# A kernel of three attention layers: normalising the outputs instead of the probabilities, with the inverse sums returned from DRAM

## The reference, cut to what matters

```
s = q @ k.T * scale                       # layer 1: masked, and one sink logit appended
p = softmax(s)                            # over the keys (and the sink)
o = p @ v
y = (o * silu(g)) @ w_o
```

## Time and profile before

| | |
|---|---|
| median of 3 runs | 1159.05 us (1158.66 to 1159.08) |
| profiled execution | 1159.5 us, its span 1157.7 us |
| TensorE busy | 1099.8 us (95%) |
| VectorE busy | 734.3 us (63%) |
| ScalarE busy | 649.0 us (56%) |
| GpSimd busy | 419.3 us (36%) |

### The profile page before, as it was taken

The page is one execution under the profiler, slowest core; times in us unless marked ns, Lnnn a source line. Parts: engine busy times, 40 slices in busy tenths (PEclk is TensorE's granted clock), DMA queues, the critical chain, the costliest instruction groups (busy, mean ns, idle before and its releaser), DMA issues.

```text
span 1157.7 us, 20235 instructions
## 1 busy us (share of the span) xinstructions
PE 1099.8 (95%) x7430; PEld 900.7 (78%) x7430; DVE 734.3 (63%) x1590; ACT 649.0 (56%) x1355; POOL 419.3 (36%) x513
## 2 busy tenths in 40 slices
PE   5999999999998899999899999999999999999996
PEld 2678778877885689877688887898878777888785
DVE  7575766676568625363787787745767775527745
ACT  5604555555556526643677777846567753457733
POOL 2633012212120334675400002416654326456781
PEclk9999999999999999999999999999999999999998
DMA  9741424322114521130201101053212403213112
GB/s 373 253 163 46 176 107 162 133 108 101 46 29 173 204 81 37 40 109 35 57 14 34 65 10 47 1 166 87 73 46 78 151 19 128 91 56 121 44 37 73
DMA packets 34253, 109.33 MB, mean 94 GB/s; under 512 B 4516, under 2 KB 7076, under 8 KB 33772
## 3 DMA queue, kind: packets, MB, share of 16 engines
q1 hardware_dynamic: 34156, 108.05, 27.7%
HBM read 101.39 MB, written 2.11 MB: 89 GB/s over the span
## 4 chain that ended last, share of the span: by engine, by line
PE 75%; DVE 12%; ACT 5%; issue 3%; POOL 2%; DMA 2%; SPq 1%; DVEq 0%; POOLq 0%; ACTq 0%
PE PS L677 31%; PE PS L660 15%; PE PS L794 8%; PE PS L782 7%; PE PS L983 6%; PE PS L1051 3%; DMA AF<-wstream 2%; PE PS L712 2%; DVE AD L2372 1%; ACT AF L1272 1%; DVE AF L2069 1%; POOL AR L2553 1%; DVE AR L2273 1%; PE PS L884 1%; PE PS L693 1%
## 5 line engine op out<-in xcount | busy, mean ns | idle before, releaser
L2553 POOL TENSOR_TENSOR AR<-AF,AR 128x256 fp32r<-128x256 f32 x396 | 304.5, 802 | 585.2 <-ACT AR L1152 585.2
L677 PE MATMUL PS<-AR 128*128 128x512 f32 (+1 forms) x2208 | 450.5, 360 | 4.7 <-POOL AR L2553 1.4
L677 PEld LDWEIGHTS PS<-AR 128*128 128x128 f32 x2208 | 364.0, 189 | 72.6 <-issue 10.5
L660 PE MATMUL PS<-AR 128*128 128x256 f32 (+4 forms) x1284 | 244.9, 327 | 6.7 <-ACT AF L1272 1.7
L660 PEld LDWEIGHTS PS<-AR 128*128 128x128 f32 (+1 forms) x1284 | 179.8, 190 | 41.7 <-issue 20.6
L1281 ACT ACTIVATE AF<-PS 128x512 f32<-128x512 f32 (+3 forms) x192 | 124.6, 649 | 100.0 <-PE PS L782 96.0
L1272 ACT ACTIVATE AF<-PS,AF 128x512 f32<-128x512 f32 (+3 forms) x192 | 140.8, 733 | 27.2 <-DVE AF L2349 18.3
L782 PE MATMUL PS<-AF 128*128 128x128 f32 x864 | 127.4, 274 | 8.4 <-DVE AF L1990 5.9
L782 PEld LDWEIGHTS PS<-AF 128*128 128x128 f32 x864 | 100.1, 140 | 32.9 <-issue 15.5
L1152 ACT ACTIVATE AR<-AF 128x1024 fp32r<-128x1024 f32 x99 | 103.3, 1052 | 35.3 <-PE PS L983 27.9
L794 PE MATMUL PS<-AF 128*64 128x128 f32 x1728 | 115.3, 278 | 3.4 <-DVE AF L1997 2.5
(11 more groups left out here) (216 smaller groups left out, 1147.2 us busy)
## 6 DMA issues: line engine op xcount, KB each, us to landing
AF<-wstream SPq DMA_DIRECT2D x171, 512.0 KB, 5.0
AF<-x_in SPq DMA_DIRECT2D x2, 1024.0 KB, 8.5
AD<-rows SPq DMA_DIRECT2D x4, 512.0 KB, 5.9
out<-AF SPq DMA_DIRECT2D x16, 128.0 KB, 1.9
AF<-AF SPq DMA_DIRECT2D x28, 64.0 KB, 2.0
AF<-rpb_band SPq DMA_DIRECT2D x8, 224.0 KB, 5.2
BIAS<-rpb_band SPq DMA_DIRECT2D x8, 224.0 KB, 4.7
AF<-ctx_in SPq DMA_DIRECT2D x1, 1024.0 KB, 5.5
```

Source lines behind the costliest of these rows:

```text
L660: mm = pe.matmul(out, stationary, moving, start=i == 0, stop=i == len(products) - 1)
L677: mm = pe.matmul(out[:, 0:t1 - t0], a, b, start=k == 0 and i == 0, stop=k == nk - 1 and i == 2)
L2553: ins = pool.tensor_tensor(w[:, 1, at:at + 256], raw(c)[:, at:at + 256], w[:, 0, at:at + 256].bitcast(F32), ALU.subtract)
```

## The change

In the first six pairs of layer 1 and the first seven of layer 2 (`N_LATE`) the probabilities are no longer normalised. TensorE turns the bare exponentials as soon as `exp_done` says that they are there. The sums of a pair are collected (`late_sums`): 2 x 6 columns in layer 1, 2 x 4 in layer 2. At the first step of the next pair VectorE adds the sinks' part and inverts them all (`invert_sums`). The outputs have the queries on the free axis, so the inverse sums, which are columns, must become rows: SyncE stores them to DRAM element by element (each column to 128 consecutive numbers), waits until they are there, and loads them back as rows spread over 64 partitions for each half of the pair (`spread_sums`). At the first step of the pair after that VectorE multiplies the gated output by those rows (`scale_output`); in layer 2 the one of pair 6 follows at the last step of pair 7. The high parts wait for `scaled`. In the other pairs nothing changes.

```diff
+N_LATE = {"A": 6, "B": 7, "C": 0}
...
+        SUMS_AT = {"A": LOC_[:, 5920:5992], "B": ROPE[:, 1, 0:48]}
+        SUMS_OF = {layer: [tiles(SUMS_AT[layer][:, 4 * n * i:], 2, 2, n) for i in range(3)] for layer, n in (("A", 6), ("B", 4))}
+        SUM_ROWS = {"A": R3[:, 3072:3840].bitcast(F32), "B": ROPE[:, 0, :]}
...
             def turn(n):
                 u = units[n]
-                pe.wait_ge(p_ready, n + 1)
+                if late(n):
+                    pe.wait_ge(exp_done, n + 1)
+                else:
+                    pe.wait_ge(p_ready, whole_at[n] + 1)
...
+                total, sunk = late_sums(n) if late(n) else (STAT[:, 2, i:i + 1], STAT[:, 3, i:i + 1])
...
-                               accum_out=STAT[:, 2, i:i + 1]).then_inc(exp_done, 1)
+                               accum_out=total).then_inc(exp_done, 1)
...
             def out_high_a(j):
                 act.wait_ge(o_read, 2 * j + 2)
+                if j < N_LATE["A"]:
+                    act.wait_ge(scaled, late_at("A", j) + 1)
...
             def out_high_b(j, part):
                 act.wait_ge(o_read, 16 + j + 1)
+                if j < N_LATE["B"]:
+                    act.wait_ge(scaled, late_at("B", j) + 1)
...
+            def invert_sums(layer, p):
+
+                dve.wait_ge(exp_done, pair_scored(layer, p))
+                sums, sinks, inverse = (SUMS_OF[layer][i][:, p % 2] for i in range(3))
+                if layer == "A":
+                    step(dve.tensor_tensor(sums, sums, sinks, ALU.add))
+                signal(dve.reciprocal(inverse, sums), sums_ready, late_at(layer, p) + 1)
+
+            def scale_output(layer, p):
+
+                rows = SUM_ROWS[layer]
+                dve.wait_ge(sums_in, 32 * (late_at(layer, p) + 1))
+                ins = dve.tensor_tensor(OG[:, p, :], OG[:, p, :], rows[:, 0:S], ALU.mult)
+                if layer == "A":
+                    ins = dve.tensor_tensor(OGC[:, p, :], OGC[:, p, :], rows[:, S:T], ALU.mult)
+                signal(ins, scaled, late_at(layer, p) + 1)
+
+            def late_work(layer, m):
+
+                n = per_pair[layer]
+                p, s = (m - start_of[layer]) // n, (m - start_of[layer]) % n
+                if s == 0 and 1 <= p <= N_LATE[layer]:
+                    invert_sums(layer, p - 1)
+                if s == 0 and 2 <= p <= N_LATE[layer] + 1:
+                    scale_output(layer, p - 2)
+                if s == n - 1 and p == N_LATE[layer] == N_PAIR - 1:
+                    scale_output(layer, p - 1)
...
+                    if m < m1 and not late(2 * m):
                         normalise(2 * m)
                     if early and m0 <= m - 2 < m1 - 1 and units[2 * (m - 2)]["out"] is not None:
                         gate_output(m - 2)
+                    if m < m1 and not late(2 * m):
+                        normalise(2 * m + 1)
                     if m < m1:
-                        normalise(2 * m + 1)
+                        late_work("A" if early else "B", m)
...
                         turn_queries(p)
+                        if p >= 2:
+                            spread_sums("A", p - 2)
...
-                        load_roped_queries(first)
-                        load_roped_queries(first + 1)
+                        for p in (first, first + 1):
+                            load_roped_queries(p)
+                            spread_sums("B", p - 2)
+                        if p == N_PAIR - 1:
+                            spread_sums("B", p - 1)
...
+            def spread_sums(layer, p):
+
+                if p >= N_LATE[layer]:
+                    return
+                n, i = per_pair[layer], late_at(layer, p)
+                sp.wait_ge(sums_ready, i + 1)
+                sp.dma_start(sums_dram[p % 2, 0:2 * n * P].rearrange("(i q) -> q i", q=P),
+                             SUMS_OF[layer][2][:, p % 2].rearrange("p h t -> p (h t)"), allow_slow_non_contiguous=True).then_inc(sums_stored, 16)
+                sp.wait_ge(sums_stored, 16 * (i + 1))
+                if i:
+                    sp.wait_ge(scaled, i)
+                for h in range(2):
+                    sp.dma_start(SUM_ROWS[layer][ROWS_OF[h], 0:n * P],
+                                 sums_dram[p % 2:p % 2 + 1, h * n * P:(h + 1) * n * P].to_broadcast([64, n * P])).then_inc(sums_in, 16)
```

More of the change, by code:

```diff
@@ L285, in order_d, with build @@
         task(f"C.o{j}.x", bank, f"C.o{j}")
-def build(nc, wstream, cst, rope, cols, x_in, ctx_in, vbias, rpb_band, rows_dram, out):
+def build(nc, wstream, cst, rope, cols, x_in, ctx_in, vbias, rpb_band, rows_dram, sums_dram, out):
     AT, _ = column_layout()
@@ L486, in build @@
             sem("rope_queries_in0"), sem("rope_queries_in1")]
+        sums_ready, sums_stored, sums_in, scaled = (sem(n) for n in (
+            "inverse_sums", "inverse_sums_stored", "inverse_sums_in", "outputs_scaled"))
         qr_hi, qr_lo = sem("roped_query_high"), sem("roped_query_low")
@@ L592, in is_c, with late, late_at, late_sums @@
             return n >= 2 * B_END
+        def late(n):
+            return units[n]["pair"] < N_LATE[units[n]["layer"]]
+        whole = [n for n in range(len(units)) if not late(n)]
+        whole_at = {n: i for i, n in enumerate(whole)}
+        def late_at(layer, p):
+            return p + (N_LATE["A"] if layer == "B" else 0)
+        def late_sums(n):
+            u = units[n]
+            t = n // 2 - start_of[u["layer"]] - per_pair[u["layer"]] * u["pair"]
+            sums, sinks = (SUMS_OF[u["layer"]][i][:, u["pair"] % 2] for i in range(2))
+            return sums[:, u["half"], t:t + 1], sinks[:, u["half"], t:t + 1]
         def score_bank(n):
@@ L1269, in exps @@
                 i = n % 4
+                total, sunk = late_sums(n) if late(n) else (STAT[:, 2, i:i + 1], STAT[:, 3, i:i + 1])
                 if u["sink"] is not None:
-                    act.activation(STAT[:, 3, i:i + 1], u["sink"], ACT.Exp, bias=STAT[:, 1, i:i + 1])
+                    act.activation(sunk, u["sink"], ACT.Exp, bias=STAT[:, 1, i:i + 1])
                 act.activation(probs(n)[:, 0:u["c1"] - u["c0"]], score_bank(n)[:, u["c0"]:u["c1"]], ACT.Exp,
                                bias=STAT[:, 1, i:i + 1], scale=-1.0 if is_a(n) or is_c(n) else u["scale"],
-                               accum_out=STAT[:, 2, i:i + 1]).then_inc(exp_done, 1)
+                               accum_out=total).then_inc(exp_done, 1)
             def turned(n):
@@ L3032 @@
     out = nc.dram_tensor("out", (P, KD, S), F32, kind="ExternalOutput").ap()
-    build(nc, rows_dram=rows_dram, out=out, **args)
+    sums_dram = nc.dram_tensor("sums", (2, 2 * T), F32, kind="Internal").ap()
+    build(nc, rows_dram=rows_dram, sums_dram=sums_dram, out=out, **args)
     result = run_bass_kernel_spmd(nc, [arrays], core_ids=[0]).results[0]["out"]
```

## The result

The changed kernel takes 1168.13 us (median of 4 runs, 1167.74 to 1171.43), the kernel before in the same series 1159.07 us (4 runs, 1158.66 to 1160.28): a ratio of 1.0083, 95% interval 1.0063 to 1.0103, so 9 us (0.8%) slower. The forecast was 1160.4 us, with 1155.5 to 1167.0 as range. The profiled execution took 1167.74 us, with a span of 1165.9 us.

The account below looks back on a forecast made before the run. TensorE, busy 1099.8 of 1157.7 us, was taken as the bound. Waits saved, VectorE's additions and the queue's delay, −5.0 + 0.3 + 1.1 + 4.95 = +1.35 us, gave 1160.4 us, range 1155.5 to 1167.0.

Parts of the forecast that it names:

- The gain: TensorE's waits on VectorE's removed work: 3.9 us saved in layer 1, 1.1 in layer 2, 5.0 in total.
- The part of the forecast without the queue: Both layers' saved waits and the work added on VectorE: −5.0 + 0.3 + 1.1 us.
- VectorE's additions: Added inversions and output scaling: 0.3 us at layer 1's pair 6, 1.1 in its pair 7, nothing at layer 2's end.
- SyncE's queue: Layer 1's store is hidden; in layer 2's last pair chunk B.o5 waits behind pair 6's sums, delaying TensorE 4.95 us.
- 0.65 + L: TensorE's delay in layer 2's last pair, L being the time from the store's issue to its landing.
- The signs: Right if layer 1's idle falls to 2 to 3 us and TensorE idles about 5 us in layer 2's last pair.
- One sign of being wrong: The store of sums takes beyond 10 us, so that layer 1's weights come late too.
- What the store takes: Time from issue to landing of the element-by-element store of sums: 4.3 us taken, bounds 1.76 and 11.4.
- The store is slow: Rival: the store of sums takes 9 to 11.4 us to land, total 1165.1 to 1167.5 us; chance 0.20.
- the stall costs the clock too: Rival: TensorE's clock falls for one attention step in layer 2's last pair, total 1165.6 us; chance 0.10.

Follow-up runs that it names:

- layer 1 alone: Layer 1's first six pairs late, layer 2 as before the change, against the kernel before: 1157.38 us, ratio 0.9982.
- whole partitions: Changed kernel with each partition's sums stored side by side in DRAM, loads unchanged so outputs wrongly scaled: 1159.35 us, ratio 0.9994 to the kernel before.
- layer 2 alone: Layer 2's first six pairs late, layer 1 as before the change, against the kernel before: 1159.02 us, ratio 0.9994.
- the later scaling: Kernel with six late pairs in each layer, pair 5's outputs scaled in the third step of layer 1's pair 7: 1156.82 us, ratio 0.9966 to the kernel before.

## Why the prediction was wrong

**The gain** was right in size. Forecast: 3.9 us of waits in layer 1. From 6.2 to 1.7 us of idle time in the first six pairs is 4.5. Its parts came out otherwise, and that they nearly cancel is luck: the wait of 1.7 us on the exponential went whole, where 0.5 was counted, and the 0.5 on the gated output stayed as 0.4. Net of 0.3 and 1.1 for VectorE's additions the forecast for layer 1 was 2.5; the changed kernel's trace gives 2.98, the runs of layer 1 alone 2.1. Layer 2: forecast 1.1, measured 1.42 in the trace. The part of the forecast without the queue is −3.6 us. The kernel with six and six late pairs measures −3.3 (2.3 to 4.5 us faster), the one with all 13 and the last sums moved −2.3 by its ratio (1.3 to 3.4).

**VectorE's additions.** The 1.1 us in pair 7 is exact in the wait (1.74 to 2.80), but its price was less than that: the chunk behind it was awaited for 1.75 us in the kernel before. The clock fell behind this wait of 2.8 us in six of the eleven traces that have it, the changed kernel's among them (16 matmuls of L734 in 3.10 us in place of 1.91), and the fall is paid mostly from the same slack: from this group to the wait at the end of the pair it takes 20.3 us with the fall (363.14 to 383.46), 19.7 in the kernel before without it.

**SyncE's queue** went link by link as forecast: pair 6's sums, store, landing, two loads, B.o5, split, copy, transposes. The formula for the stall, 0.65 + L, holds within 0.4 us for every L from 1.41 to 4.60 and is 0.8 us short at 8.64 and 1.6 at 7.93, where the two load issues took 1.80 and 2.48 us for the 1.3 put in (the row of the forecast has 1.43 for two) and the chunk 4.6 and 4.7 us to land for the 4.1. In layer 1 the store took 9.2 to 11.1 us and cost nothing, as forecast: TensorE has no wait on a chunk from 97 to 320 us.

**The signs.** ScalarE's L1177 waits for `wstream`, 64 instances of the multiplication are left, and TensorE has its one idle piece where it was forecast, but of 10.1 and not of 5 us; the idle time of the first six pairs fell to 1.7, somewhat below the 2 to 3. One sign of being wrong came half: stores took beyond 10 us, but layer 1's weights were not late. The profile gives no landing for these stores, so L is read from the store's issue to the first load's.

**The step that failed** is the term "What the store takes": 4.3 us chosen, 8.64 measured, inside the bounds of 1.76 to 11.4. By it alone the forecast would have been 1160.4 + 4.3 = 1164.7 us. (By the terms as I wrote them, 1.57 + 2.6, it would have been 4.2; this decides nothing.) The reasoning was of the wrong kind. I spread the cost over 64 packets per engine at a price read from rows of 1 KB; but a quarter of the packets costs nearly the same, and the packets are through long before the store is. The stretch from 726 to 737 us, cut in 40 slices, shows the busy share of the DMA engines in tenths:

```profile
DMA  0000000772000000000000002000700000000000
```

Three slices, 0.8 us, hold the store's packets; then nothing moves for 3.8 us, and the two busy slices after that are fetches of instructions (one packet each of the queues for instructions). The estimate that I worked out from the Trainium skill's price per packet (DMA: Bandwidth & Descriptors, section Bandwidth), L near 2.5 us, fits these packets and comes near the store with numbers 64 bytes apart (2.85), and misses this one by 6 us. The same page's advice against a strided last dimension (Rules for kernel authors) stands, for a dearer reason than the number of descriptors: 1.41 us by whole partitions, 8.64 as single numbers.

**The second step that failed** is the list of rivals: two of them were priced as alternatives. "The store is slow" (0.20, up to 1167.5 us) and "the stall costs the clock too" (0.10, 1165.6 us) are one event here: behind the long stall the clock fell. Their sum, 1164.7 plus 2.5 for the clock, is 1167.2, and with the 0.8 us missing from the formula 1168.0, beside 1168.13 measured. That it meets so closely is luck too: in the two traces the gain is 4.3 us (2.98 and 1.3) and not 3.6. The Trainium skill (TensorE: Matmul & The Clock Gate, Part 1) says of an idle TensorE what the windows above show: 1.00 before the stall, 0.50 behind it, and 1.00 again only after it has worked.

## What to carry to other kernels

A wait put into a queue that runs in order is priced by what stands behind it there: the same 13 pairs cost 9 us or gain 2, by the place of one call among SyncE's issues. A transfer's price is not that of its packets: where many partitions write single numbers side by side, ask for the time to its landing, and if no row has it, plan as if it were the upper bound. And price a long stall and the clock behind it together: here 10.1 us of stall brought 2.5 us more. The version to keep is the one with six late pairs in either layer, 1156.4 us, 0.3% (0.2 to 0.4) faster than the kernel before.

## What the runs showed of the hardware

- A store of 1024 numbers of 4 bytes from 128 partitions, neighbours side by side in DRAM, takes 8.6 to 11.1 us from its issue to that of the load that waits for it, though its packets pass in 0.8 us; 256 such numbers still take 7.9 to 9.5. At distances of 8, 16 and 64 bytes, with the other distances spread alike, the 1024 take 4.6, 3.2 and 2.9 us in the last pair, as 128 pieces of 32 bytes 1.4.
- TensorE's clock was at 1.2 GHz behind idle times of 10.1, 5.1 and 2.4 us (transposes in 1.51 us in place of 0.85), and in one trace behind 2.06 us (five transposes in 1.27 us in place of 0.71). Behind one of 2.8 us in layer 1 it fell in six of eleven traces, as in the changed kernel's (3.10 in place of 1.91 us), and not in the other five, as in that of the kernel with six and six late pairs. Behind the one of 1.74 us it did not fall in any of the three kernels whose traces have it (before, layer 2 alone, the later scaling).
